# Expert weights in transfers of 2 MiB with four rows per partition, and gate and up products that take every fourth column

## The chip, the core and the metric

The kernel runs on one core of a Trainium2 chip. The metric is the time of one execution on the device in microseconds; three runs are taken and their median is given. One further execution was taken with the hardware profiler, and the rows below come from it.

## The reference

The model is two blocks on a sequence of 256 tokens of width 1024, all in f32. The first is two layers (a short convolution and a block attention, each followed by an attention to a memory of 256 rows and a gated feed-forward of width 2816). The second is one layer whose gates and shifts come from a modulation vector, with a gated delta rule branch and a latent attention branch side by side, and then a mixture of experts in which each expert chooses its tokens. The change touches only this last part and what prepares its gain and bias:

```python
def expert_choice_ffn(h, w_router, w_gate, w_up, w_down):
    bsz, s, d = h.shape
    cap = CAPACITY_FACTOR * s // N_EXPERTS          # 32 tokens for each of 16 experts
    aff = jax.nn.softmax((h @ w_router).astype(jnp.float32), axis=-1)
    gate, idx = lax.top_k(aff.transpose(0, 2, 1), cap)
    idx_flat = idx.reshape(bsz, N_EXPERTS * cap)
    xe = jnp.take_along_axis(h, idx_flat[..., None], axis=1).reshape(bsz, N_EXPERTS, cap, d)
    hid = jax.nn.silu(jnp.einsum('becd,edf->becf', xe, w_gate)) * jnp.einsum('becd,edf->becf', xe, w_up)
    ye = jnp.einsum('becf,efd->becd', hid, w_down) * gate[..., None].astype(h.dtype)
    out = jnp.zeros_like(h).at[jnp.arange(bsz)[:, None], idx_flat].add(ye.reshape(bsz, N_EXPERTS * cap, d))
    return out
```

Each of w_gate, w_up and w_down has 16 matrices of 1024 x 1024 f32, 4 MiB each: 192 MiB in all. The h that goes in is the normalised row times a gain (1 + sc2) g_ffn and plus a bias sh2, which come from the modulation.

## The kernel before, in words

Every engine has its own list of operations, written out by hand in program order, and semaphores between the lists. The dense layers stream their weights through a ring of four places: SP loads 1 MiB, ScalarE and VectorE split it into two parts (lines 243 and 250), TensorE multiplies (lines 424 to 426 and 440 to 442).

The expert weights take another way. They are cut into 192 chunks of 1 MiB: chunk j of a matrix is its rows 256j to 256j+255, two consecutive rows (8 KiB) per partition. `order()` gives the sequence: the four gate chunks and the four up chunks of an expert, then the four down chunks of the expert before it. There are 22 places of 8 KiB per partition (`wexp`), scattered over SBUF where earlier buffers come free; chunk n goes to place n mod 22. `load_expert` (line 2498) issues one chunk on SP's queue. The first 22 wait for the earlier owners of their places: three in `early_experts`, four beside the chunks of w_out (`next_experts`), the rest in `sp_experts`. From chunk 22 on SP waits until TensorE has used the chunk that lies in the place (`e_used`, raised once per chunk).

`expert_chunk` (line 2718) multiplies a chunk. The 32 chosen tokens of the expert are the stationary operand, 32 columns wide, and the weights are the moving one; the 1024 output columns are cut into four groups of 256, each of which goes to its own 32 columns of the array and its own 32 partitions of PSUM, so that four products run side by side. An f32 product leaves two records in the trace, so a chunk (two rows k, four groups c) leaves 16. The group c is the 256 consecutive columns from 256c on:

```python
dst[32 * c:32 * c + 32, :], lhs(2 * j + kk), wexp[n_ % NSLOT][:, kk, c * W4:(c + 1) * W4]
```

Which rows of a matrix lie in which partition sets what goes with them. Since partition p holds rows 2p and 2p+1 of a chunk, the gathered input (line 2735, products of the split rows with the 0/1 selection) takes every second column of each 256, and so do the turned hidden rows (line 2809), the gain and the bias (`xgain`, `xbias`, made in `modulation_rows`, lines 1228 to 1247, and from `vpair`, lines 927 to 934).

The order of the work around it: SP's queue holds the loads in the order of the chunks; TensorE's list first has the products with w_out, the router, filler products that nobody reads (`unread`, line 2565), then 16 gathers for two halves of the experts. The first four gate chunks stand between gathers (`first_gate`), the rest behind them (`pe_experts`). For each expert it then goes: gate and up; down of the expert before; turning the hidden rows. In the last two experts fillers stand behind each chunk. After the last down product the last output product (line 2827) and the final norm follow (`finish`).

Of the kernel before, what the change touches and what calls it, by code (L numbers as in the profile page):

```python
# [87 lines left out]
def build(nc, A, out):  # L88
# [423 lines left out]
    vpair = place("vpair", [12, 256], F32, offset=F0 + 34368)  # L512
# [19 lines left out]
    def load_vectors(e):  # L532
        for n_, k_ in VROWS[1:]:
            src = A[n_]
            flat = src.rearrange(" ".join("abc"[:len(src.shape)]) + " -> (" + " ".join("abc"[:len(src.shape)]) + ")")
            e.dma_start(vrow[vat[n_]:vat[n_] + k_, 0, :], flat.rearrange("(k p) -> k p", p=P)).then_inc(misc, 16)
        w5 = A["conv_w_2"][0].rearrange("w (k p) -> (w k) p", p=P)
        e.dma_start(vrow[0:CONV2 * 24, 1, :], w5).then_inc(misc, 16)
        e.dma_start(vrow[0:48, 2, :], A["b_mod_2"].rearrange("a (k p) -> (a k) p", p=P)).then_inc(misc, 16)
        for j, v_ in enumerate((A["b_mod_2"][:, 3 * D:4 * D], A["b_mod_2"][:, 4 * D:5 * D], A["g_ffn_2"])):  # L540
            e.dma_start(vpair[4 * j:4 * j + 4, :], v_.rearrange("a (c n) -> (a c) n", c=4)).then_inc(misc, 16)
# [390 lines left out]
    by_pair = V0[:, 296:320].rearrange("p (h j c) -> p j c h", h=2, j=3)  # L932
    for j, dst in enumerate((bpair[:, 0:8], bpair[:, 8:16], xgain)):
        dve.do(lambda e, j=j, dst=dst: e.tensor_copy(dst.rearrange("p (c h) -> p c h", h=2), by_pair[:, j, :, :]))
# [291 lines left out]
    def modulation_rows(prepared):  # L1226
# [16 lines left out]
        pv = X[0][:, 2 * P:4 * P].rearrange("p (h c v) -> p v c h", h=2, c=4)  # L1243
        ch2 = lambda v_: v_.rearrange("p (c h) -> p c h", h=2)
# [1213 lines left out]
    for c in range(1, 4):  # L2458
# [9 lines left out]
        for _ in half:  # L2468
# [6 lines left out]
    NSLOT = 22  # L2475
    first = st.n + 4
    ring_at = [sbuf_at[f"{n_}{(first + i) % RING}"] for i in range(RING) for n_ in ("w_raw", "w_hi")]
    wexp = [place(f"w_exp{i}", [P, 2, D], F32, offset=at)
            for i, at in enumerate((F0 + 24576, F0 + 32768, A0 + 16384, A0 + 24576, A0 + 32768, S0, S0 + 24576,
                                    S0 + 8192, S0 + 16384, A0, A0 + 8192, *ring_at, A0 + 40960, XN, sbuf_at["x"]))]  # L2480
    e_in = [nc.alloc_semaphore(f"expert_in{s_}") for s_ in range(NSLOT)]

# [13 lines left out]
    def load_expert(e, n_):  # L2496
        name, x_, j = list(order())[n_]
        e.dma_start(wexp[n_ % NSLOT][:, :, :],
                    A[name][0][x_][256 * j:256 * j + 256, :].rearrange("(p k) n -> p k n", k=2)).then_inc(e_in[n_ % NSLOT], 16)
# [211 lines left out]

    def expert_chunk(e, name, x_, j, dst, lhs):

        n_ = chunk_at[name, x_, j]
        e.wait_ge(e_in[n_ % NSLOT], 16 * (n_ // NSLOT + 1))
# [33 lines left out]
    NCH = 12 * E  # L2749
# [4 lines left out]
    def sp_experts(e):  # L2754
        for n_ in range(7, NCH):
            if n_ == 7:
                e.wait_ge(*t_merged)
            elif 11 <= n_ < 19:
                e.wait_ge(S["chunk_used"], RING + first - 4 + (n_ - 11) // 2 + 1)
            elif n_ == 19:  # L2760
                e.wait_ge(*t_x1)
            elif n_ == 20:
                e.wait_ge(*t_rows[1])
            elif n_ == 21:
                e.wait_ge(*t_held)
                e.wait_ge(*x_read[1])
            elif n_ >= NSLOT:
                e.wait_ge(e_used, n_ - NSLOT + 1)
            load_expert(e, n_)
    sp.raw(sp_experts)  # L2770

    def pe_experts(e):
# [11 lines left out]
        def down(x_):  # L2784
# [9 lines left out]
            for j in range(4):  # L2794
                expert_chunk(e, "w_down_2", x_, j, into[:, 0:W4], lambda k: hT[x_ % 2][:, k % 2, (k // 2) * C:(k // 2 + 1) * C])
# [5 lines left out]
        def turn_hidden(x_):  # L2801
# [6 lines left out]
            for c in range(2):  # L2808
                ins = e.transpose(XT[:, c * P:(c + 1) * P], hx[x_ % 2][:, :].rearrange("p (q h) -> p h q", h=2)[:, c, :], ident[:, :])
# [146 lines left out]
```

## Time and profile before

| what | value |
|---|---|
| three runs | 1763.61, 1770.14, 1771.63 us (median 1770.14) |
| profiled execution | 1778.02 us |
| its span, first to last instruction | 1776.3 us |
| mean granted TensorE clock | 0.937 |
| TensorE busy | 1583.8 us (89%) |
| DMA traffic over the span | 417 MB, 235 GB/s |
| loads of expert weights | 192 of 1 MiB, 26.6 to 27.0 us from issue to landing (median) |

The span is cut into 40 slices in the page, so a slice is 44.4 us. The busy share of an engine is an average over stages with different limits; the stage of the expert weights fills the last 12 slices.

### The profile page before, as it was taken

How to read it: one execution, taken by the hardware profiler on the slowest of the kernel's cores; microseconds unless marked ns; L12 is line 12 of the kernel's file. 1: busy time of each engine (PE TensorE's matmuls, PEld its weight loads, DVE VectorE, ACT ScalarE, POOL GpSimd, SP SyncE). 2: the span in 40 equal slices, each digit the busy share in tenths (PEclk: the TensorE clock that was granted, in tenths of full speed). 3: DMA queues.
4: the chain of work that ended last, by engine and by line, in shares of the span. 5: the costliest groups of instructions: out<-in, count | busy, mean ns of one | idle time of the engine just before them, and what ended most of it. 6: DMA issues, size and time to landing. Idle time of an engine off the chain costs nothing.

```text
span 1776.3 us, 35258 instructions
## 1 busy us (share of the span) xinstructions
PE 1583.8 (89%) x14826; PEld 1317.4 (74%) x14826; DVE 865.3 (49%) x1248; ACT 661.2 (37%) x884; POOL 143.3 (8%) x188
## 2 busy tenths in 40 slices
PE   8999999999999999999989799899999666666677
PEld 8999899988989989988888689789885222222223
DVE  5765466645655556564667589866651000000001
ACT  5445354435444435543545644534442000000001
POOL 5700000000000000000105001121110000000000
PEclk9999999999999999999999999999999776777779
DMA  7765556775735666655544144102699999999997
GB/s 247 252 200 186 183 155 189 218 255 165 262 120 178 231 186 200 182 175 174 148 123 149 58 143 143 50 27 73 239 412 403 421 421 421 420 421 421 420 421 304
DMA packets 254141, 417.17 MB, mean 235 GB/s; under 512 B 15102, under 2 KB 215345, under 8 KB 229425
## 3 DMA queue, kind: packets, MB, share of 16 engines
q1 hardware_dynamic: 253825, 414.59, 65.4%
q8 instruction: 109, 1.79, 0.4%
q10 hardware_dynamic: 176, 0.53, 0.1%
q14 instruction: 31, 0.25, 0.0%
HBM read 414.04 MB, written 1.05 MB: 234 GB/s over the span
## 4 chain that ended last, share of the span: by engine, by line
issue 47%; PE 41%; DVE 5%; POOL 4%; ACT 3%; DMA 0%; DVEq 0%; POOLq 0%; ACTq 0%; SPq 0%
PE bank L424 4%; PE bank L425 4%; PE bank L426 4%; PE bank L440 2%; PE bank L442 2%; PE bank L441 2%; PE bank L1878 2%; DVE cy L1427 1%; PE bank L1079 1%; PE bank L1078 1%; PE bank L1077 1%; PE bank L759 1%; PE bank L452 1%; POOL ang L908 1%; POOL ang L909 1%
## 5 line engine op out<-in xcount | busy, mean ns | idle before, releaser
L250 DVE TENSOR_TENSOR w_lo<-w_raw,w_hi 128x2048 fp32r<-128x2048 f32 (+2 forms) x178 | 400.8, 2254 | 252.7 <-ACT w_hi L243 252.6
L243 ACT ACTIVATE w_hi<-w_raw 128x2048 fp32r<-128x2048 f32 (+2 forms) x178 | 334.0, 1880 | 155.6 <-DMA w_raw<-in_ffn_w_down_dram 57.7
L424 PE MATMUL bank<-h_hi,w_hi 128*128 128x256 f32 x1168 | 328.0, 281 | 5.1 <-DVE h_lo L637 3.8
L425 PE MATMUL bank<-h_lo,w_hi 128*128 128x256 f32 x1168 | 327.2, 280 | 0.0
L426 PE MATMUL bank<-h_hi,w_lo 128*128 128x256 f32 x1168 | 327.2, 280 | 0.0
L2718 PE MATMUL bank<-w_exp,xeT 128*32 128x256 f32 x2048 | 170.9, 473 | 79.9 <-DMA w_exp<-in_w_up_dram 51.3
L424 PEld LDWEIGHTS bank<-h_hi,w_hi 128*128 128x128 f32 x1168 | 222.8, 191 | 6.2 <-issue 6.1
L426 PEld LDWEIGHTS bank<-h_hi,w_lo 128*128 128x128 f32 x1168 | 219.6, 188 | 0.0
L425 PEld LDWEIGHTS bank<-h_lo,w_hi 128*128 128x128 f32 x1168 | 219.4, 188 | 0.0
L2718 PEld LDWEIGHTS bank<-w_exp,xeT 128*32 128x32 f32 x2048 | 65.7, 128 | 177.6 <-DMA w_exp<-in_w_up_dram 84.3
L2718 PE MATMUL bank<-w_exp,hT 128*32 128x256 f32 x1024 | 93.9, 504 | 47.6 <-DMA w_exp<-in_w_down_dram 47.6
L2885 DVE TENSOR_TENSOR hx<-sg,bank 128x256 f32<-128x256 f32 x16 | 6.7, 421 | 255.2 <-ACT sg L2857 255.2
L2718 PEld LDWEIGHTS bank<-w_exp,hT 128*32 128x32 f32 x1024 | 34.5, 134 | 104.4 <-DMA w_exp<-in_w_down_dram 62.0
L440 PE MATMUL bank<-w_hi,a_hi 128*128 128x256 f32 x384 | 107.9, 281 | 1.1 <-issue 1.1
L442 PE MATMUL bank<-w_hi,a_lo 128*128 128x256 f32 x384 | 107.2, 279 | 0.0
L441 PE MATMUL bank<-w_lo,a_hi 128*128 128x256 f32 x384 | 107.2, 279 | 0.0
L2857 ACT ACTIVATE sg<-bank 128x256 f32<-128x256 f32 x16 | 6.1, 383 | 256.8 <-PE bank L2718 256.8
L2893 DVE TENSOR_TENSOR ye<-bank,gt 32x256 f32<-32x256 f32 x64 | 26.9, 420 | 135.3 <-PE bank L2718 134.6
L440 PEld LDWEIGHTS bank<-w_hi,a_hi 128*128 128x128 f32 x384 | 72.0, 188 | 1.4 <-issue 1.3
L441 PEld LDWEIGHTS bank<-w_lo,a_hi 128*128 128x128 f32 x384 | 72.1, 188 | 0.1
L442 PEld LDWEIGHTS bank<-w_hi,a_lo 128*128 128x128 f32 x384 | 72.0, 188 | 0.0
L1079 PE MATMUL bank<-w_hi,a_lo 128*128 128x512 f32 x176 | 69.4, 394 | 0.0
(539 smaller groups left out, 3084.8 us busy)
## 6 DMA issues: line engine op xcount, KB each, us to landing
w_exp<-in_w_gate_dram SPq DMA_DIRECT2D x64, 1024.0 KB, 26.6
w_exp<-in_w_up_dram SPq DMA_DIRECT2D x64, 1024.0 KB, 26.6
w_exp<-in_w_down_dram SPq DMA_DIRECT2D x64, 1024.0 KB, 27.0
w_raw<-in_ffn_w_gu_dram SPq DMA_DIRECT2D x88, 512.0 KB, 5.0
w_raw<-in_w_in_dram SPq DMA_DIRECT2D x54, 512.0 KB, 4.8
w_mod<-in_w_mod_dram SPq DMA_DIRECT2D x24, 1024.0 KB, 7.1
w_raw<-in_ffn_w_down_dram SPq DMA_DIRECT2D x44, 512.0 KB, 4.2
w_raw<-in_mem_w_kv_dram SPq DMA_DIRECT2D x32, 512.0 KB, 4.6
```

Source lines behind the costliest of these rows:

```text
L243: e.activation(whi[slot][:, 0:w], raw[slot][:, 0:w], ACT.Copy).then_inc(S["hi_ready"], 1)
L250: e.tensor_tensor(wlo[slot][:, 0:w], raw[slot][:, 0:w], whi[slot][:, 0:w].bitcast(F32), ALU.subtract).then_inc(S["lo_ready"], 1)
L424: e.matmul(dst, whi[slot][:, lo:hi_], bh[:, k, :], start=begin, stop=False)
L425: e.matmul(dst, whi[slot][:, lo:hi_], bl[:, k, :], start=False, stop=False)
L426: ins = e.matmul(dst, wlo[slot][:, lo:hi_], bh[:, k, :], start=False, stop=end)
L440: e.matmul(dst, bh[:, k, xs], w0, start=(k == 0), stop=False)
L441: e.matmul(dst, bh[:, k, xs], w1, start=False, stop=False)
L442: ins = e.matmul(dst, bl[:, k, xs], w0, start=False, stop=(k == kts - 1))
L1079: ins = e.matmul(dst, xl, w0, start=False, stop=(k == 2 * n - 1))
L1878: tok = pe.do(lambda e, cs=cs, s_=s_: e.matmul(out_bank[cs, s_ * 64:s_ * 64 + 64], lhs[cs, s_, :], rhs[cs, s_, :], start=True, stop=True), *w)
L2718: ins = e.matmul(dst[32 * c:32 * c + 32, :], lhs(2 * j + kk), wexp[n_ % NSLOT][:, kk, c * W4:(c + 1) * W4], start=(j == 0 and kk == 0), st ...
L2893: ins = e.tensor_tensor(ye[32 * (x_ % 4):32 * (x_ % 4) + 32, x_ // 4 % 2, c * W4:(c + 1) * W4], from_[32 * c:32 * c + 32, 0:W4], gt[32 * c ...
```

## The change

Two neighbouring chunks of a matrix become a pair: 512 rows, of which partition p holds the four rows 4p to 4p+3, 16 KiB in a run. The 22 places are regrouped into 11 pairs (`pair_of`): ten are two places that lie side by side in SBUF, the eleventh is two places apart. A pair is one transfer of 2 MiB, except for the first 22 chunks, for pairs that go to the eleventh, split place, and for the very last pair: these are loaded as two halves of 1 MiB, each with two of a partition's four rows. The first 22 halves are issued in the order in which the places come free, as before, but the chunk that belongs to a place is now another (`chunk_of`), so they are not issued in the order of their use. SP waits for both chunks of a pair to be used before it loads the next. TensorE waits for the pair's semaphore.

With four rows to a partition, everything that goes with the rows is taken in fours: the gathered input takes every fourth column of each 512, gain and bias likewise. For the hidden rows the change does it on the other side: in gate and up products, group c is no longer 256 consecutive columns but the columns 4q + c, and the hidden rows can then be turned without a step; down products keep consecutive columns. In `modulation_rows` two transposes become eight products of 64 output partitions into another bank, and the three VectorE operations on them become six, on half the partitions each.

```diff
-    pairs = vpair[:, :].rearrange("r (p h) -> r h p", h=2)
-    for h in range(2):
-        t = pe.do(lambda e, h=h: e.transpose(V0[:, 296 + 12 * h:308 + 12 * h], pairs[:, h, :], ident[0:12, 0:12]))
+    fours = vpair[:, :].rearrange("r (p h) -> r h p", h=4)
+    for h in range(4):
+        t = pe.do(lambda e, h=h: e.transpose(V0[:, 296 + 6 * h:302 + 6 * h], fours[:, h, :], ident[0:6, 0:6]))
...
-        for h in range(2):
-            tp = pe.do(lambda e, h=h: e.transpose(X[0][:, (2 + h) * P:(3 + h) * P], mrow[:, :].rearrange("p (q h) -> p h q", h=2)[:, h, :],
-                                                  ident[:, :]))
+        for h in range(4):
+            for a_ in range(2):
+                t4 = pe.do(lambda e, h=h, a_=a_: e.matmul(X[3][64 * a_:64 * a_ + 64, h * P:(h + 1) * P],
+                                                          mrow[:, :].rearrange("p (q h) -> p h q", h=4)[:, h, :], ident[:, :],
+                                                          start=True, stop=True), xfree[3])
...
-        t = dve.do(lambda e: e.tensor_tensor(ch2(xbias), pv[:, 4, :, :], ch2(bpair[:, 8:16]), ALU.add), tp, t)
-        t = dve.do(lambda e: e.scalar_tensor_tensor(out=xgain, in0=xbias, scalar=1.0, in1=xgain, op0=ALU.add, op1=ALU.mult), t)
-        t = dve.do(lambda e: e.tensor_tensor(ch2(xbias), pv[:, 3, :, :], ch2(bpair[:, 0:8]), ALU.add), t)
+        for a_ in range(2):
+            fs = slice(64 * a_, 64 * a_ + 64)
...
+            t = dve.do(lambda e, pv=pv, ch4=ch4: e.tensor_tensor(ch4(xbias), pv[:, 4, :, :], ch4(bpair[:, 8:16]), ALU.add), t4, t)
+            t = dve.do(lambda e, fs=fs: e.scalar_tensor_tensor(out=xgain[fs, :], in0=xbias[fs, :], scalar=1.0, in1=xgain[fs, :],
+                                                               op0=ALU.add, op1=ALU.mult), t)
+            t = dve.do(lambda e, pv=pv, ch4=ch4: e.tensor_tensor(ch4(xbias), pv[:, 3, :, :], ch4(bpair[:, 0:8]), ALU.add), t)
...
+    def pair_rows(m):
+        name, x_, j = list(order())[2 * m]
+        return A[name][0][x_][256 * j:256 * j + 512, :].rearrange("(p k) n -> p k n", k=4)
+
+    def load_half(e, n_, sem):
+        e.dma_start(wexp[n_ % NSLOT][:, :, :], pair_rows(n_ // 2)[:, n_ % 2 * 2:n_ % 2 * 2 + 2, :]).then_inc(sem, 16)
+
+    def load_expert(e, i):
+        load_half(e, chunk_of[i], e_in[chunk_of[i]])
+
+    def load_pair(e, m):
+        if m == NCH // 2 - 1:
+            for hf in range(2):
+                load_half(e, 2 * m + hf, e_in[hf])
+        elif m % NP == NP - 1:
+            for hf in range(2):
+                load_half(e, 2 * m + hf, pair_in[m % NP])
+        else:
+            e.dma_start(wpair[m % NP][:, :, :], pair_rows(m)).then_inc(pair_in[m % NP], 16)
...
+    def group_of(name, row, c):
+        return row[:, c * W4:(c + 1) * W4] if name == "w_down_2" else row.rearrange("p (q c) -> p c q", c=4)[:, c, :]
...
-                               wexp[n_ % NSLOT][:, kk, c * W4:(c + 1) * W4],
+                               group_of(name, wexp[n_ % NSLOT][:, kk, :], c),
...
-                X[b][:, 0:H * C], part[:, t_, (k // 2) * 256:(k // 2 + 1) * 256].rearrange("p (q h) -> p h q", h=2)[:, k % 2, :], Sa[:, t_, cs],
+                X[b][:, 0:H * C], part[:, t_, (k // 4) * 512:(k // 4 + 1) * 512].rearrange("p (q h) -> p h q", h=4)[:, k % 4, :], Sa[:, t_, cs],
...
-            elif n_ >= NSLOT:
-                e.wait_ge(e_used, n_ - NSLOT + 1)
-            load_expert(e, n_)
+            load_expert(e, i)
+        for m in range(NP, NCH // 2):
+            e.wait_ge(e_used, 2 * (m - NP) + 2)
+            load_pair(e, m)
...
-                ins = e.transpose(XT[:, c * P:(c + 1) * P], hx[x_ % 2][:, :].rearrange("p (q h) -> p h q", h=2)[:, c, :], ident[:, :])
+                ins = e.transpose(XT[:, c * P:(c + 1) * P], hx[x_ % 2][:, c * P:(c + 1) * P], ident[:, :])
```

## Rows read from the trace of the kernel before

**Rows 1.** The page, the span in 40 equal slices.

```profile
PE   8999999999999999999989799899999666666677
PEclk9999999999999999999999999999999776777779
DMA  7765556775735666655544144102699999999997
```

**Rows 2.** The chain that ended last: start us, us, what.

```profile
1326.05 444.46 issue
```

**Rows 3.** Windows by stage.

```profile
core 0: us, PE busy (x) PEld busy (x) DVE busy (x) ACT busy (x) POOL busy (x), PEclk, DMA share, GB/s
1265.00:1340.00 75.00, 70.72 (x579) 63.72 (x578) 39.55 (x70) 31.98 (x49) 6.24 (x5) 1.00 1.03 402
...
1400.00:1440.00 40.00, 24.96 (x262) 8.80 (x264) 2.11 (x5) 0.77 (x2) 0.00 (x0) 0.74 1.01 421
1440.00:1750.00 310.00, 211.00 (x2066) 80.28 (x2067) 21.44 (x51) 8.05 (x21) 0.00 (x0) 0.75 1.01 421
```

**Rows 4.** Waits of SP, 1200 to 1777: us in total, times, longest us.

```profile
SPq L2498 <- PE bank L2718: 203.3, 153, 4.5
```

**Rows 5.** The page: packets; queue 1 (packets, MB, share of 16 engines); one row of issues.

```profile
DMA packets 254141, 417.17 MB, mean 235 GB/s; under 512 B 15102, under 2 KB 215345, under 8 KB 229425
...
q1 hardware_dynamic: 253825, 414.59, 65.4%
...
w_exp<-in_w_gate_dram SPq DMA_DIRECT2D x64, 1024.0 KB, 26.6
```

**Rows 6.** Timeline of TensorE in the tail: start us, us.

```profile
1752.31 1.07 PE L2718 MATMUL bank<-w_exp,hT 128*32 128x256 f32 x16 [1.80 <-DMA w_exp<-in_w_down_dram]
...
1754.80 1.94 PE L2718 MATMUL bank<-w_exp,hT 128*32 128x256 f32 x16 [0.22 <-DMA w_exp<-in_w_down_dram]
...
1758.73 1.07 PE L2718 MATMUL bank<-w_exp,hT 128*32 128x256 f32 x16
...
1764.67 1.07 PE L2718 MATMUL bank<-w_exp,hT 128*32 128x256 f32 x16 [0.85 <-DMA w_exp<-in_w_down_dram]
...
1766.82 3.60 PE L2827 MATMUL bank<-ye,GT 128*128 128x512 f32 x8
```

**Rows 7.** Timeline of TensorE behind the gathers: chunks 4 to 7.

```profile
1342.06 3.66 PE L2718 MATMUL bank<-w_exp,xeT 128*32 128x256 f32 x64
```

**Rows 8.** Timeline of SP's issues there, and times to landing from 1320 to 1345.

```profile
1326.08 0.81 SPq L2498 DMA_DIRECT2D w_exp<-in_w_gate_dram  x2
...
1331.13 2.74 SPq L2498 DMA_DIRECT2D w_exp<-in_w_gate_dram  x2
...
1343.19 1.94 SPq L2498 DMA_DIRECT2D w_exp<-in_w_up_dram  x2
...
DMA to landing us min/median/max: 5.3/7.6/9.6
```

**Rows 9.** A window of one microsecond, columns as in rows 3.

```profile
1344.00:1345.00 1.00, 1.00 (x24) 0.63 (x20) 0.00 (x0) 0.24 (x2) 0.00 (x0) 1.00 0.89 205
```

**Rows 10.** Single lines: weight loads in sequence and with a step, ns min/median/max.

```profile
L1230 PEld LDWEIGHTS bank<-ident,mrow x2: 137/138/138, 790.6 to 790.7; 128*128 128x128 f32 x2
...
L1232 PEld LDWEIGHTS bank<-ident,mrow x2: 195/201/207, 790.8 to 790.9; 128*128 128x128 f32 x2
...
L2735 PEld LDWEIGHTS bank<-Sa,h_hi x32: 193/195/198, 1328.0 to 1341.6; 128*128 128x128 f32 x32
```

**Rows 11.** The page, groups: busy us, mean ns of one, idle before.

```profile
L424 PEld LDWEIGHTS bank<-h_hi,w_hi 128*128 128x128 f32 x1168 | 222.8, 191 | 6.2 <-issue 6.1
```

**Rows 12.** Timeline of all engines at the modulation: start us, us.

```profile
793.73 0.17 DVE L1245 TENSOR_TENSOR small<-bank,bpair 128x8 f32<-128x8 f32 x1
793.93 0.17 DVE L1246 SCALAR_TENSOR_TENSOR small<-small 128x8 f32<-128x8 f32 x1
...
795.05 1.95 PE L1254 MATMUL bank<-mexp,sel 128*128 128x512 f32 x4 [2.04 <-DVE gt L1256]
```

More of the change, by code:

```diff
@@ L511, in build @@
     vrow = place("vrow", [P, 3, P], F32, offset=F0 + 32832)
-    vpair = place("vpair", [12, 256], F32, offset=F0 + 34368)
+    vpair = place("vpair", [6, 512], F32, offset=F0 + 34368)
     def col(name, k=0):
@@ L540, in load_vectors @@
         for j, v_ in enumerate((A["b_mod_2"][:, 3 * D:4 * D], A["b_mod_2"][:, 4 * D:5 * D], A["g_ffn_2"])):
[L541 removed]
+            e.dma_start(vpair[2 * j:2 * j + 2, :], v_.rearrange("a (c n) -> (a c) n", c=2)).then_inc(misc, 16)
         e.dma_start(invf[:, :], A["inv_freq"]).then_inc(pos_in, 16)
@@ L2474, in build @@
     E, C = N_EXP, CAP
-    NSLOT = 22
+    NSLOT, NCH = 22, 12 * E
     first = st.n + 4
     ring_at = [sbuf_at[f"{n_}{(first + i) % RING}"] for i in range(RING) for n_ in ("w_raw", "w_hi")]
-    wexp = [place(f"w_exp{i}", [P, 2, D], F32, offset=at)
-            for i, at in enumerate((F0 + 24576, F0 + 32768, A0 + 16384, A0 + 24576, A0 + 32768, S0, S0 + 24576,
-                                    S0 + 8192, S0 + 16384, A0, A0 + 8192, *ring_at, A0 + 40960, XN, sbuf_at["x"]))]
+    NP = NSLOT // 2
+    free_in_order = (F0 + 24576, F0 + 32768, A0 + 16384, A0 + 24576, A0 + 32768, S0, S0 + 24576,
+                     S0 + 8192, S0 + 16384, A0, A0 + 8192, *ring_at, A0 + 40960, XN, sbuf_at["x"])
+    pair_of = [next((i, j) for i in range(NSLOT) for j in range(NSLOT)
+                    if free_in_order[i] == a_ and free_in_order[j] == a_ + 8192)
+               for a_ in (F0 + 24576, A0 + 16384, S0, S0 + 16384, A0, *(min(free_in_order[i], free_in_order[i + 2]) for i in (11, 12, 15, 16)), A0 + 32768)] + [(20, 21)]
+    chunk_of = {i: 2 * m + hf for m, two in enumerate(pair_of) for hf, i in enumerate(two)}
+    wpair = [place(f"w_exp_pair{m}", [P, 4, D], F32, offset=free_in_order[two[0]]) for m, two in enumerate(pair_of[:-1])]
+    wexp = [wpair[m][:, 2 * hf:2 * hf + 2, :] for m in range(NP - 1) for hf in range(2)]
+    wexp += [place(f"w_exp{i}", [P, 2, D], F32, offset=free_in_order[i]) for i in pair_of[-1]]
     e_in = [nc.alloc_semaphore(f"expert_in{s_}") for s_ in range(NSLOT)]
+    pair_in = [nc.alloc_semaphore(f"expert_pair_in{m}") for m in range(NP)]
     def order():
@@ L2494, in order, with landed @@
             yield "w_down_2", E - 1, j
[L2496 to L2499, printed above, removed]
+    def pair_rows(m):
[14 more added lines that the diff above has]
+            e.dma_start(wpair[m % NP][:, :, :], pair_rows(m)).then_inc(pair_in[m % NP], 16)
+    def landed(n_):
+        m = n_ // 2
+        if n_ < NSLOT:
+            return e_in[n_], 16
+        if m == NCH // 2 - 1:
+            return e_in[n_ % 2], 32
+        return pair_in[m % NP], (32 if m % NP == NP - 1 else 16) * (m // NP)
     def early_experts(e):
@@ L2754, in sp_experts @@
     def sp_experts(e):
-        for n_ in range(7, NCH):
-            if n_ == 7:
+        for i in range(7, NSLOT):
+            if i == 7:
                 e.wait_ge(*t_merged)
-            elif 11 <= n_ < 19:
-                e.wait_ge(S["chunk_used"], RING + first - 4 + (n_ - 11) // 2 + 1)
-            elif n_ == 19:
+            elif 11 <= i < 19:
+                e.wait_ge(S["chunk_used"], RING + first - 4 + (i - 11) // 2 + 1)
+            elif i == 19:
                 e.wait_ge(*t_x1)
-            elif n_ == 20:
+            elif i == 20:
                 e.wait_ge(*t_rows[1])
-            elif n_ == 21:
+            elif i == 21:
                 e.wait_ge(*t_held)
                 e.wait_ge(*x_read[1])
-            elif n_ >= NSLOT:
-                e.wait_ge(e_used, n_ - NSLOT + 1)
-            load_expert(e, n_)
+            load_expert(e, i)
+        for m in range(NP, NCH // 2):
+            e.wait_ge(e_used, 2 * (m - NP) + 2)
+            load_pair(e, m)
     sp.raw(sp_experts)
@@ L2794, in down @@
             for j in range(4):
-                expert_chunk(e, "w_down_2", x_, j, into[:, 0:W4], lambda k: hT[x_ % 2][:, k % 2, (k // 2) * C:(k // 2 + 1) * C])
+                expert_chunk(e, "w_down_2", x_, j, into[:, 0:W4], lambda k: hT[x_ % 2][:, k // 4, (k % 4) * C:(k % 4 + 1) * C])
                 if x_ == E - 2:
```

12 lines of the change are left out of this document (6 added, 6 removed).

## The prediction

> **What bounds the kernel now.** I read the slices of the page first. For the first 28 of the 40 slices TensorE is busy nine tenths and the DMA engines anything from nothing to nine tenths; from slice 29 on, the stage of the expert weights, the picture turns over: the DMA engines stand at nine tenths and TensorE falls to six or seven [rows 1]. The chain that ended last is of no use in this stage: it has one step of 444.46 us called "issue" from 1326.05 to the tail [rows 2], because it does not follow the transfer queue. So the windows by stage decide: from 1400 to 1750 us all 16 DMA engines are busy (share 1.01) and move 421 GB/s, in both windows alike, while TensorE works 25 of 40 us at three quarters of its clock [rows 3]. The queue is never short of a place either: SP waits 203 us there for TensorE to hand places back [rows 4], and a load lands 26.6 us after its issue, ten loads deep [rows 5]. A load of 1.0486 MB at 421 GB/s takes 2.49 us, and 2.49 us is also the distance at which TensorE's waits for the last loads end (1752.31, 1754.80) [rows 6]. The end of the kernel is therefore: the moment at which the DMA engines begin to run full (about 1265), plus the bytes over the rate, plus every hole in the DMA traffic, plus what TensorE does after the last load (from 1764.67). The change has to be priced in these four places, and in TensorE's path before 1265.
>
> **The rate: 77 loads of 2 MiB.** Of 192 chunks the first 22 still come singly, as do the two chunks of the split place in each round (7 pairs) and the last pair. 96 - 11 - 7 - 1 = 77 pairs become one transfer. The transfers before have 8 KiB per packet: 24,716 packets (254,141 less 229,425) are of 8 KB or more, and 192 loads times 128 partitions are 24,576 [rows 5]. What one packet costs comes from two sums. Queue 1 was busy 65.4% of 16 x 1776.3 us = 18,587 us. The expert loads have 201.3 MB of it, at 421 GB/s and share 1.01: 7,728 us in 24,576 packets. The rest is 213.3 MB and 10,859 us in 229,249 packets. Solving for a price per MB and one per packet gives 36.8 us per MB (16 engines: 435 GB/s) and 13.1 ns per packet. Some 3 ns of that overlap the next packet, since the share reads 1.01 and not 1.00 of 314 ns, so 10 ns count in time. A full pair has 8 packets of 16 KiB per engine instead of 16 of 8 KiB: 8 x 10 = 80 ns saved, times 77 = **-6.2 us**. Bounds: 0 (if a long row is cut again into pieces of 8 KiB, nothing is saved), and -12.4 us (if 154 MiB ran at the full 435 GB/s: 154 x (2.491 - 2.410)). The 402 GB/s of 1265 to 1340, where rows of 1 KiB for w_out are mixed in [rows 3], say that packets do cost something, so I take the middle one. The Trainium skill (DMA: Bandwidth & Descriptors, Why small descriptors are slow) has about 3 cycles a packet and 32 bytes of descriptor, which at its fabric clock is some 4.7 ns; by that the gain would be only about 2.9 us.
>
> **The hole around 1344.** This is where the release in pairs is felt. Chunks 20 and 21 are issued by 1326.5, chunk 22 at 1331.13 when chunk 0 is used, 23 at 1333.5, and so on, and 26 only at 1343.19, since the first gate chunks lie between the gathers and chunk 4 comes behind them at 1342.06 [rows 7, 8]. Loads in this stretch land 5.3 us after issue at least, so a load begins some 1.6 us after its issue when nothing stands ahead, and there the traffic falls to 205 GB/s for a microsecond [rows 8, 9]. Before, chunk 25 is through at about 1344.2. Going back four loads at 402 GB/s, chunk 21 is through at about 1333.8. After, chunks 22 and 23 wait for chunk 1 (1333.5) and start at 1335.1: through at 1340.1; 24 and 25 wait for chunk 3 (1338.35), through at 1345; 26 and 27 wait for chunk 5, 1344.06 instead of 1343.19, and start at 1345.7 instead of 1344.8. **+0.9 us**, and whatever delays chunk 5 on TensorE adds to it one for one. After that pairs are released every 1.7 us against 4.9 us of transfer, and nothing is lost.
>
> **Columns with a step of four.** The moving operand of gate and up is now read at a step of 16 bytes. No matmul before reads a moving operand with a step; the nearest rows are weight loads: the same 128x128 of f32 takes 138 ns in sequence and 201 ns with a step of 8 bytes, 1.4 to 1.5 times, while the gather's split weights with a step of two take 195 ns [rows 10], against 191 ns for split weights in sequence [rows 11]. A chunk is 16 matmul records in 0.9 us at full clock (64 in 3.66) [rows 7]. I take 1.4 times, +0.36 us a chunk, since these are unsplit f32 as in the first pair of rows; the bounds are no cost and, if the four column groups had to read one after the other, 4 times. In the steady stage this is covered: (2 x 1.3 + 0.9) / 3 is 1.2 us a chunk against 2.49, and even at the low clock (1.94 us a chunk at 1754.80 [rows 6]) it is 2.5, with the clock free to rise. Up to chunk 5 it is not: six chunks, 6 x 0.36 = **+2.2 us**. The gather's 64 weight loads go from a step of two to four: between 0 and 64 x 57 ns = 3.6 us; the split weights show 4 ns for step two, so **+0.3 us**. The Trainium skill (SBUF — State Buffer, the door of the DMA port swizzle, its note on cachelines of 16 bytes) wants at least two hits per line for full speed, which this read of f32 no longer has; that speaks against the change, and its consequence is the first rival.
>
> **The tail.** Chunk 186 landed for 1752.31, 187 for 1754.80; now both land with 187. TensorE then has, in a row: 186 (1.9, the low clock) and four filler products (1.2), 187 (1.1) and four (0.9), turning the hidden rows until 188 can start (1.2), 188 to 190 with fillers (1.6, 1.9, 1.5): 11.3 us, read from the starts of the chunks [rows 6] and of the fillers between them. The last half lands 9.9 us after that pair. **+1.3 us**; bounds 0 and, if the clock stays at 1.2 GHz there and in the 3.60 us of the output product, +8.
>
> **Modulation, near 791 us.** Two transposes go, eight f32 products of 128 columns come (16 records at some 60 to 110 ns, 1 to 1.8 us). The engine behind them waits 2.04 us for VectorE anyway [rows 12], which covers them; without that cover they would cost up to 1.8. VectorE's chain gets three more operations of 0.17 us with 0.03 between them, ahead of the gt products on which that wait rests [rows 12]: **+0.6 us**. The vector transposes early on (four for two, of six rows) are under 0.2 us. The step in the transposes of hidden rows goes away: 2 x 0.06 us, off the path. SP issues fewer transfers; it waits anyway. The new order of the first 22 loads puts chunk 18 at the fifth place and brings chunks 4 to 7 later, but all of them stand ahead of the issue at 1326.08 [rows 8], and chunk 4 is first used at 1342.06 [rows 7].
>
> **Sum.** -6.2 + 0.9 + 2.2 + 0.3 + 1.3 + 0.6 = -0.9 us. The profiled execution took 1778.0 us around a span of 1776.3, so it would be 1777.1; the median of the three runs is 1770.1, and it would be **1769.2**. About 0.5% (8.9 us) is what a measurement of this kernel can tell from no change, so this is "within".
>
> **Rivals.** (1) *The strided read becomes slow enough to show*, the other side. With d us more per gate or up chunk, the start costs 6d. Near the end each of expert 15's eight gate and up chunks carries 1.0 us of fillers too, so 0.9 + 1.0 + d exceeds 2.49 from d = 0.5 to 0.6 on, and eight of them pile up 8(d - 0.5), of which the four down chunks win back 1.9. At d = 1.8 (3 times) that is 10.8 + 8.5 against the 2.2 in the sum: +17, **1786**. Slower by 0.5% from about d = 1.3, 2.4 times. For it: sequence against step in the weight loads, and four column groups reading at once. Against: the split weights hardly mind. Chance 0.20. (2) *The strided read is free*: -3.1 us, **1767**. 0.20. (3) *Long rows save nothing*, the change not doing what it says: +5.3, **1775**. 0.12. (4) *Long rows run at 435 GB/s and the read is free*: -12.4 + 0.9 + 0.3 + 1.3 + 0.6 = -9.3, **1761**, just faster. For it only the round figure that the solution gave. 0.10. (5) *The clock falls in the tail* because TensorE now idles once per pair for longer: +7 to +8, **1777**, at times over the line. 0.06. The forecast keeps 0.32.
>
> Faster: (4), and a little of (2) = 0.13. Slower: (1) and some of (3) and (5) = 0.23. Within: 0.64. The range takes in (4) and (1) up to three times: 1759 to 1786; the forecast's own is 1764 to 1775.
>
> **What would show it.** The steady windows: 427 to 428 GB/s if a packet costs 10 ns, 421 if nothing is saved. The number of packets: 9,856 fewer. Sixteen matmuls of a gate chunk at full clock: 1.3 us against 0.9. The traffic between 1333 and 1346: two holes of about a microsecond. The start of the last chunk, against the last landing: over a microsecond late. The prediction falls if rates in the steady windows go down (16 KiB rows in step across partitions), or if a gate chunk takes over 2.2 us.

## The result, and the profile after

The changed kernel took 1785.7 us (median of nine runs) against 1770.2 us for the kernel before (nine runs): a ratio of **1.0081 [1.0065, 1.0097]**, 14.3 us slower. The prediction was 1769.2 us and no change to be told. The ratios here and below rest on undisturbed executions alone; two of the twelve of e12 took 2991.6 and 3770.7 us, for a reason that no trace shows, and stand outside its ratio.

The two profiled executions lie only 3.5 us apart in their spans (1779.8 against 1776.3), because that of before was a late one: at the modulation, near 790 us, it stood 5.8 us behind the other, and there the two kernels have run the same work but for two tiny transposes more in the changed kernel. So I compare stretches that begin at a common mark. The mark for the stage of the experts is the first start of the operation that writes xn behind the last residual (line 2649 before, line 2686 after). This is the view of that line in the changed kernel:

```profile
core 0 of [0], span 1779.8 us
...
L2686 ACT ACTIVATE xn<-x,small x2: 1132/1132/1133, 1314.9 to 1317.0; 128x1024 f32<-128x1024 f32 x2
```

From 1314.9 to the end of the span are 464.9 us. Before they were 456.2 us (1320.1 to 1776.3): **+8.7 us** in this stage.

The page of the changed kernel, slices, packets and queue 1, answering to [rows 1] and [rows 5]:

```profile
PE   9999999999999999999989799899999977686778
PEclk9999999999999999999999999999999999998999
DMA  7755657765736557645453244002898999999996
...
DMA packets 243040, 417.15 MB, mean 234 GB/s; under 512 B 13864, under 2 KB 214095, under 8 KB 228181
...
q1 hardware_dynamic: 242725, 414.59, 64.8%
```

Three windows of the changed kernel (columns as in [rows 3]): two of the places where traffic all but stops, and the steady stage. Behind them the same steady window of the kernel before:

```profile
1330.00:1332.00 2.00, 2.00 (x17) 0.60 (x10) 0.00 (x0) 0.44 (x1) 0.00 (x0) 1.00 0.10 41
1348.00:1350.00 2.00, 2.00 (x21) 0.60 (x16) 0.00 (x0) 0.64 (x2) 0.00 (x0) 1.00 0.00 0
...
1450.00:1700.00 250.00, 178.19 (x1659) 62.38 (x1652) 18.01 (x43) 6.69 (x18) 0.00 (x0) 0.93 1.01 427
```

```profile
1450.00:1700.00 250.00, 167.63 (x1608) 60.62 (x1605) 18.50 (x44) 6.52 (x17) 0.00 (x0) 0.72 1.01 421
```

The reader sees three things. The packets are fewer by 11,101: 9,856 because 16 KiB now go in one packet instead of two, and the rest are small ones that the 77 transfers fewer no longer need. The steady rate is 427 GB/s for 421, as forecast. But between 1328 and 1352 the traffic falls away three times, near 1331, 1340 and 1349, while TensorE is busy without a break in the windows shown; the middle time it does not stop (33 GB/s in its lowest microsecond). And in the steady stage TensorE works longer for the same products: 178 of 250 us at a granted clock of 0.93, against 168 us at 0.72.

TensorE's timeline of the changed kernel at the first gate chunks, answering to [rows 7], and SP's issues there, answering to [rows 8]:

```profile
1325.77 2.00 PE L2758 MATMUL bank<-w_exp_pair,xeT 128*32 128x256 f32 x16
1327.69 0.51 PE L2775 MATMUL bank<-Sa,h_hi 128*128 128x256 f32 x1
1328.04 0.39 PE L2775 MATMUL bank<-Sa,h_lo 128*128 128x256 f32 x1
1328.27 0.40 PE L2775 MATMUL bank<-Sa,h_hi 128*128 128x256 f32 x1
...
1346.46 7.45 PE L2758 MATMUL bank<-w_exp_pair,xeT 128*32 128x256 f32 x64
```

And the first gate chunk of the kernel before, with the gather's products behind it:

```profile
1330.00 1.07 PE L2718 MATMUL bank<-w_exp,xeT 128*32 128x256 f32 x16 [0.15 <-ACT xeT L2738]
1331.00 0.39 PE L2735 MATMUL bank<-Sa,h_hi 128*128 128x256 f32 x1
1331.23 0.28 PE L2735 MATMUL bank<-Sa,h_lo 128*128 128x256 f32 x1
1331.35 0.28 PE L2735 MATMUL bank<-Sa,h_hi 128*128 128x256 f32 x1
```

SP's issues in the changed kernel:

```profile
1331.82 0.33 SPq L2528 DMA_DIRECT2D w_exp_pair<-in_w_gate_dram  x1
...
1339.85 0.33 SPq L2528 DMA_DIRECT2D w_exp_pair<-in_w_up_dram  x1
...
1350.36 0.33 SPq L2528 DMA_DIRECT2D w_exp_pair<-in_w_up_dram  x1
```

Sixteen products of a gate chunk take 1.92 us from the first to the next operation (1325.77 to 1327.69), and 1.00 us before (1330.00 to 1331.00); 64 of them take 7.45 us for 3.66. The gather's products follow each other at 0.23 us, and before at 0.12. All of this lies ahead of chunk 5, whose use releases the third pair: it is issued 35.5 us after the mark (1350.36), and chunk 26 before was issued 23.1 us after it. The transfer queue has run dry by then. I call *missing traffic* the sum of (1 less GB/s over the steady rate) over the windows of one microsecond that lie below the steady rate in the first 60 us behind the mark: **14.6 us** after, 2.6 us before.

### The profile page after: what moved, and what is told of

Its sections match the earlier page's. It is cut to its first block, busy times and chain, and to the rows that moved or that the text cites. A ratio compares the mean times of both kernels' runs of the same rounds, so it can differ in the third digit from the quotient of the medians.

```text
span 1779.8 us, 35217 instructions
## 1 busy us (share of the span) xinstructions
PE 1628.3 (91%) x14842; PEld 1323.0 (74%) x14842; DVE 865.6 (49%) x1251; ACT 662.7 (37%) x884; POOL 149.5 (8%) x188
## 4 chain that ended last, share of the span: by engine, by line
issue 47%; PE 40%; DVE 5%; POOL 4%; ACT 3%; DMA 1%; DVEq 0%; POOLq 0%; SPq 0%; ACTq 0%
PE bank L424 4%; PE bank L425 4%; PE bank L426 4%; PE bank L440 2%; PE bank L442 2%; PE bank L441 2%; PE bank L1884 2%; PE bank L1077 1%; PE bank L1079 1%; PE bank L1078 1%; PE bank L759 1%; DVE cy L1433 1%; POOL ang L908 1%; PE bank L452 1%; POOL ang L909 1%
## 5 line engine op out<-in xcount | busy, mean ns | idle before, releaser
L2758 PE MATMUL bank<-w_exp_pair,xeT 128*32 128x256 f32 x1888 | 223.3, 631 | 40.4 <-DMA w_exp_pair<-in_w_gate_dram 22.5
L2758 PEld LDWEIGHTS bank<-w_exp_pair,xeT 128*32 128x32 f32 x1888 | 65.7, 126 | 181.1 <-issue 134.1
L2758 PE MATMUL bank<-w_exp_pair,hT 128*32 128x256 f32 x928 | 64.9, 425 | 37.6 <-DMA w_exp_pair<-in_w_down_dram 37.6
L2758 PEld LDWEIGHTS bank<-w_exp_pair,hT 128*32 128x32 f32 x928 | 32.1, 120 | 72.1 <-DMA w_exp_pair<-in_w_down_dram 31.9
L1077 PE MATMUL bank<-w_hi,a_hi 128*128 128x512 f32 x176 | 69.7, 396 | 0.0
```

Source lines behind the costliest of these rows:

```text
L1077: e.matmul(dst, xh, w0, start=(k == 0), stop=False)
```

## The experiments

Each of e1 to e12 was timed against the kernel before on the same chip, with twelve executions of its own (e11 with six); e13 and e14 were only profiled. The kernels e1 to e6, e10 and e14 leave out the reordering that one side of a product would need, so they do the same amount of work but do not compute the reference. The table has the ratio with its interval; the stage of the experts from the mark to the end in the profiled execution; the missing traffic; the steady rate; and the idle time marked issue in front of TensorE's first product of line 465.

| run | ratio | stage, us | missing, us | GB/s | line 465, us |
|---|---|---|---|---|---|
| before | 1 | 456.2 | 2.6 | 421 | 1.3 |
| the change | 1.0081 [1.0065, 1.0097] | 464.9 | 14.6 | 427 | 2.5 |
| e1_flat_groups | 1.0029 [1.0009, 1.0049] | 456.9 | 8.6 | 427 | 2.4 |
| e2_flat_gather | 1.0037 [1.0018, 1.0056] | 460.1 | 9.1 | 427 | 2.6 |
| e3_flat_both | 1.0001 [0.9983, 1.0020] | 454.0 | 5.2 | 427 | 2.3 |
| e4_before_step | 1.0030 [1.0010, 1.0049] | 462.1 | 7.0 | 421 | 1.3 |
| e5_flat_halves | 1.0031 [1.0016, 1.0046] | 461.3 | 3.9 | 421 | 2.7 |
| e6_before_modulation | 1.0030 [1.0011, 1.0050] | 456.7 | 1.5 | 421 | 2.9 |
| e7_no_steps | 1.0019 [1.0003, 1.0036] | 456.9 | 6.2 | 427 | 2.7 |
| e8_no_steps_ends | 1.0006 [0.9990, 1.0022] | 454.1 | 5.0 | 426 | 2.7 |
| e9_more_records | 1.0016 [1.0001, 1.0032] | 456.8 | 1.4 | 421 | 1.5 |
| e10_fewer_records | 1.0011 [0.9989, 1.0033] | 457.4 | 2.4 | 421 | 1.2 |
| e11_after_no_fillers | 1.0061 [1.0039, 1.0082] | 465.6 | 15.0 | 427 | 2.9 |
| e12_best | 0.9993 [0.9972, 1.0014] | 453.8 | 3.9 | 427 | 1.4 |
| e13_seam48 | not timed | 456.3 | 1.3 | 421 | 2.6 |
| e14_seam24 | not timed | 457.1 | 1.3 | 421 | 1.6 |

The row of a stage is one profiled execution. How far such a number scatters can be read from six kernels whose work in this stage is the same (before, e6, e9, e10, e13, e14): 456.2 to 457.4 us, and 1.3 to 2.6 us of missing traffic.

**e1, e2, e3: reads in order, one at a time and both.** On the changed kernel:

```diff
-        return row[:, c * W4:(c + 1) * W4] if name == "w_down_2" else row.rearrange("p (q c) -> p c q", c=4)[:, c, :]
+        return row[:, c * W4:(c + 1) * W4]
```

```diff
-                X[b][:, 0:H * C], part[:, t_, (k // 4) * 512:(k // 4 + 1) * 512].rearrange("p (q h) -> p h q", h=4)[:, k % 4, :], Sa[:, t_, cs],
+                X[b][:, 0:H * C], part[:, t_, k * P:(k + 1) * P], Sa[:, t_, cs],
```

> This is the changed kernel with one part taken back: gate and up products read consecutive columns again (so the hidden columns come out in another order than the down products want; the amount of work is the same). Theory 1, that reads with a step of 16 bytes on TensorE cost the time: a gate chunk takes 1.0 us instead of 1.9, which takes 6 us out of the hole in the DMA traffic before 1352 and the backlog of about 4 us out of the tail, so about 10 us less than the changed kernel, 1.003 of the kernel before. Theory 2, that the hand-over in pairs costs the time: no more than 1 us less, still 1.008.

> The changed kernel with the gather alone reading consecutive columns of the rows (so the gathered input has its columns in another order; the amount of work is the same). Theory 1: 64 products at 0.12 us instead of 0.23, 7 us less in the hole, 1.004 to 1.005 of the kernel before, with the gate chunks still at 1.9 us and the tail still late. Theory 2: still 1.008.

> The changed kernel with consecutive reads both in the gate and up products and in the gather (order of columns as in the two runs before, the same amount of work); transfers, places and hand-over are those of the change. Theory 1: all of the loss goes and the gain of the rate of 6 us stays, less about 3 us for holes, tail and modulation: 0.998 of the kernel before, 427 GB/s in the steady windows. Theory 2: still 1.005 or more.

Each alone takes somewhat over half of the loss away, both together all of it. The 0.998 expected for both was a little too low: the measured interval begins at 0.9983. The columns in order (e1) save 8.0 us of the stage, 6.0 of them in missing traffic; the gather in order (e2) saves 4.8, 5.5 in missing traffic. Expected were 10 and 7 us. The weight loads of the gather, single line, with the step of four (e1) and in order (e2), ns min/median/max:

```profile
L2775 PEld LDWEIGHTS bank<-Sa,h_hi x32: 307/329/332, 1328.9 to 1348.2; 128*128 128x128 f32 x32
```

```profile
L2775 PEld LDWEIGHTS bank<-Sa,h_hi x32: 186/187/192, 1322.7 to 1340.0; 128*128 128x128 f32 x32
```

With a step of two they took 195 ns [rows 10]: for these split weights a step of 8 bytes is next to free (195 ns for 187), and one of 16 bytes costs three quarters more (329 ns).

**e4: the step alone, on the kernel before.** One line of `expert_chunk` of the kernel before:

```diff
-                               wexp[n_ % NSLOT][:, kk, c * W4:(c + 1) * W4],
+                               (wexp[n_ % NSLOT][:, kk, c * W4:(c + 1) * W4] if name == "w_down_2" else wexp[n_ % NSLOT][:, kk, :].rearrange("p (q c) -> p c q", c=4)[:, c, :]),
```

> The kernel before with one part of the change alone: gate and up products read every fourth column (the hidden columns come out in another order than the down products want; the same amount of work). Loads of 1 MiB and single hand-over stay. Theory 1: a gate chunk takes 1.9 us, +6 us in the hole, and +1 to 2 us in the tail since eight chunks of 2.83 us with fillers stand against 2.49: 1.004 to 1.005 of the kernel before. Theory 2: 1.000.

1.0030 [1.0010, 1.0049], near what the theory of the slow reads had (1.004 to 1.005), and against the theory of the hand-over in pairs, since this kernel has no pairs. The stage is 5.9 us longer. The 1 to 2 us expected in the tail did not come: here the last chunk starts 0.7 us behind the last traffic, as before. Its timeline of TensorE at the first gate chunks:

```profile
1325.18 2.00 PE L2718 MATMUL bank<-w_exp,xeT 128*32 128x256 f32 x16
1328.52 2.00 PE L2718 MATMUL bank<-w_exp,xeT 128*32 128x256 f32 x16 [0.18 <-ACT xeT L2738]
```

**e5: the rate.** On e3, each full pair is loaded as two halves on the pair's semaphore:

```diff
-            e.dma_start(wpair[m % NP][:, :, :], pair_rows(m)).then_inc(pair_in[m % NP], 16)
+            for hf in range(2):
+                load_half(e, 2 * m + hf, pair_in[m % NP])
```

> As the run with both reads consecutive (same order of columns as there), but each full pair is loaded in two transfers of 1 MiB with 8 KiB per partition, handed over together as before. Theory, that the gain comes from fewer and longer packets (10 ns each): the steady windows fall from 427 back to 421 GB/s and the stage of the experts gets 6.2 us longer, 1.0035 of the kernel before. Rival, that the rate rose because SP hands out places in pairs or issues less often: 427 GB/s stays, 1.000.

The steady window of e3 and that of e5:

```profile
1450.00:1700.00 250.00, 151.00 (x1666) 68.81 (x1670) 18.49 (x44) 6.51 (x17) 0.00 (x0) 0.79 1.01 427
```

```profile
1450.00:1700.00 250.00, 149.59 (x1628) 67.47 (x1632) 16.83 (x40) 6.13 (x16) 0.00 (x0) 0.77 1.01 421
```

The rate goes back to 421 and the stage is 7.3 us longer. So the gain is real and it comes with the longer packets (and the fewer small ones), not with the way in which places are handed out. Of the 7.3 us, 6.0 are a later end of the traffic (447.5 for 441.5 us behind the mark, in windows of 0.1 us). The other 1.3 us lie in the tail, where e5 shows what the prediction had described: chunk 186 waits for the landing of its pair, TensorE then takes 1.93 us over it for the 1.07 of the others (granted clock 0.51 in those 1.9 us), and the last chunk starts 11.3 us later, 2.2 us behind the last traffic (0.9 in e3):

```profile
1759.41 1.93 PE L2759 MATMUL bank<-w_exp_pair,hT 128*32 128x256 f32 x16 [2.28 <-DMA w_exp_pair<-in_w_down_dram]
...
1770.67 1.07 PE L2759 MATMUL bank<-w_exp_pair,hT 128*32 128x256 f32 x16
```

**e6, e9, e10, e13, e14: the modulation.** In e1, e2 and e3 the timed ratios lie 2 to 4 us above what the profiled stages say. e6 is the kernel before with the change in `modulation_rows`, `vpair` and what reads it, and nothing else:

> The kernel before with only the part of the change in the modulation and its vectors (eight products and six VectorE operations for two transposes and three; gain and bias then come out in an order that the old gather does not want; the same amount of work). If this part costs what its rows say, +0.8 us, 1.0005 of the kernel before. If the 2 to 4 us by which the timed ratios of the three runs on the changed kernel lie above their profiled stages of the experts come from here, 1.002.

It was 1.0030, 5.3 us, though the stretch from the modulation to the seam is 67.4 us long for 66.6: the 0.8 us of its rows. The next thing that stands out is a wait of TensorE that the profile marks issue, that is, one for which it names nobody. Timeline of e6:

```profile
935.42 0.36 PE L465 MATMUL bank<-w_hi,h_hi 128*128 128x256 f32 x1 [2.87 <-issue]
```

It is 2.3 to 2.9 us in every kernel with the modulation part and with 32 fillers at the seam, and 1.3 before and in e4. The runs that follow vary how many TensorE products stand ahead of it, counted in records of the trace (an f32 product of the modulation leaves two, a transpose or a filler one). e9 repeats two transposes of the kernel before, 14 more products:

```diff
-        for h in range(2):
+        for h in 8 * (0, 1):
             tp = pe.do(lambda e, h=h: e.transpose(X[0][:, (2 + h) * P:(3 + h) * P], mrow[:, :].rearrange("p (q h) -> p h q", h=2)[:, h, :],
```

e10 is e6 with fewer fillers at the seam, e14 is e6 with `unread_at_seam(24)`, and e13 is the kernel before with `unread_at_seam(48)`:

```diff
-    unread_at_seam(32)
+    unread_at_seam(16)
```

> The kernel before with the two transposes of the modulation at line 1232 repeated eight times, 14 more TensorE instructions of the same kind and nothing else. Every profile of a kernel with the modulation part of the change has a stall of 2.3 to 2.9 us in front of the first product of line 465 near 935 us, which the profile calls issue, and neither profile without that part has it. Theory, that the stall comes and goes with the number of TensorE instructions ahead of it: it appears here, and the time is +0.8 and +2.6 us, 1.002. Rival, that it belongs to the modulation's operations themselves: no stall, 1.0005.

> The kernel before with the modulation part of the change, and 16 instead of 32 filler products at the seam behind it, so that as many TensorE products stand ahead of line 465 as before the change (columns in the wrong order for the old gather, as before). Theory of the count: the stall at line 465 is gone, and the ratio falls from 1.003 to 1.0005 or 1.001. Rival: it stays, 1.003. The fillers lie in a wait, so fewer of them save nothing by themselves.

> The kernel before with 48 instead of 32 filler products at the seam, nothing else: 16 TensorE products more ahead of line 465, as many as the modulation part of the change adds. Theory, that the stall marked issue in front of line 465 depends on the number of TensorE instructions ahead of it: it is 2.3 to 2.9 us long here instead of 1.3. Rival, that it depends on the modulation's own operations: 1.3.

> The kernel before with the modulation part of the change and 24 filler products at the seam: 8 products more ahead of line 465 than before. Theory of the count: 1.3 to 1.5 us, as with 0 and with 14 more. Rival: 2.3 to 2.9.

The waits of TensorE in this stretch, from the profiles of e6, e9, e10, e13 and e14:

```profile
PE bank L465 <- issue: 2.9, 1, 2.9
```

```profile
PE bank L465 <- issue: 1.5, 1, 1.5
```

```profile
PE bank L465 <- issue: 1.2, 1, 1.2
```

```profile
PE bank L465 <- issue: 2.6, 1, 2.6
```

```profile
PE bank L465 <- issue: 1.6, 1, 1.6
```

By the number of TensorE products ahead of this line beyond those of before: 0 gives 1.3 (before, e4), 1.2 (e10) and 1.4 (e12), 8 gives 1.6, 14 gives 1.5, 16 gives 2.6 (e13), 2.9 (e6) and 2.3 to 2.9 in the others. My expectation for e9 missed by two products. But e13, which has nothing of the modulation and only fillers more, has the long wait, and e10, which has all of the modulation, has not: the wait goes with the count of the products ahead, not with what they are. What happens at the count is not shown; the profile only says that TensorE waited for nothing that it records.

Nor is it shown that this wait costs the kernel its length. From the modulation (line 1230) to the mark, the kernels with the short wait took 528.5 to 530.6 us and those with the long one 529.5 to 534.1, so the two groups overlap; e6 took the most (534.1 for 529.4 before), and the changed kernel 530.0. The intervals of e6 and of e10, which has the short wait (1.0011 [0.9989, 1.0033]), overlap too. Counting 0.8 us for the rows, 1.6 for the wait and 0.5 in the stage makes 2.9 us for e6, which is inside its interval (1.9 to 8.9 us); the rest of its 5.3 us is open.

**e11: the fillers of the last expert.** On the changed kernel, in `gate_up`:

```diff
-                    if x_ == E - 1:
-                        unread(e, XG[E % 2], 4, Sa[:, 0, 0:384])
```

> The changed kernel without the four filler products behind each gate and up chunk of the last expert (work that nobody reads). Theory, that the tail is late because 1.92 us of product and 0.9 us of fillers are more than the 2.45 us in which a chunk lands: the backlog is gone, TensorE waits for the last loads again, and the last chunk starts 4 us sooner against the start of the stage: 1.006 of the kernel before. Rival, that the backlog comes from the hand-over in pairs, or that the clock falls without the fillers: nothing won, 1.008.

The changed kernel's tail, timeline of TensorE, answering to [rows 6]:

```profile
1743.34 2.00 PE L2758 MATMUL bank<-w_exp_pair,xeT 128*32 128x256 f32 x16
1745.26 0.98 PE L2602 MATMUL bank<-Sa 128*128 128x384 f32 x4
1746.17 2.00 PE L2758 MATMUL bank<-w_exp_pair,xeT 128*32 128x256 f32 x16
...
1754.64 1.07 PE L2758 MATMUL bank<-w_exp_pair,hT 128*32 128x256 f32 x16
...
1768.15 1.07 PE L2758 MATMUL bank<-w_exp_pair,hT 128*32 128x256 f32 x16
```

Chunks with fillers are 2.83 us apart, with no wait for a load from 1734.85 to the end. And that of e11:

```profile
1767.99 1.07 PE L2758 MATMUL bank<-w_exp_pair,hT 128*32 128x256 f32 x16 [0.83 <-DMA w_exp_pair<-in_w_down_dram]
...
1772.99 1.07 PE L2758 MATMUL bank<-w_exp_pair,hT 128*32 128x256 f32 x16
```

TensorE waits for loads again, so the backlog is gone; but the last chunk starts 454.0 us behind the mark and not sooner than in the changed kernel (453.3), because here the last loads themselves came later (traffic ends 453.1 us behind the mark for 451.2; the gather began 0.9 us later, for one). The expected 4 us did not come. Timed, it is 1.0061, below the changed kernel's 1.0081, with intervals that overlap. What the backlog is worth is read from how long after the last traffic the last chunk starts: 2.1 us in the changed kernel, 0.9 in e11 and 0.7 before, so 1.2 to 1.4 us.

**e7, e8, e12: the idea without slow reads on TensorE.** These compute the reference in full. On the changed kernel the normalised rows are laid down in fours by ScalarE, so the gather reads in order; gate and up read in order; and the hidden rows are turned by products that pick every fourth column in the stationary operand:

```diff
+            for k in range(4):
+                for a_ in range(2):
+                    ins = e.matmul(XT[64 * a_:64 * a_ + 64, k * 64:(k + 1) * 64],
+                                   hx[x_ % 2][:, :].rearrange("p (q k) -> p k q", k=4)[:, k, :],
+                                   ident[:, :].rearrange("p (j a s) -> p a j s", j=2, a=2)[:, a_, :, :], start=True, stop=True)
...
-        act.do(lambda e: e.activation(x_hi[:, t_, :], x[:, t_, :], ACT.Copy, scale=rs[:, t_:t_ + 1]), t_rs, all_used())
+        act.do(lambda e: e.activation(in_fours(x_hi[:, t_, :]), by_fours(x[:, t_, :]), ACT.Copy, scale=rs[:, t_:t_ + 1]), t_rs, all_used())
```

e8 also loads and hands over the first and the last three pairs behind the early ones chunk by chunk. e12 is e8 with ScalarE reading in order and writing with the step, and with `unread_at_seam(16)`.

> A full version of the idea without slow reads: pairs and 2 MiB as in the change; ScalarE writes the normalised rows already in fours, so the gather reads consecutive columns; gate and up read consecutive columns; the hidden rows are turned by eight small products with a step in the stationary operand, some 1 us per expert. Theory 1: as with both reads consecutive, the stage of the experts about 454 us, plus 0 to 2 us if ScalarE reads with a step of 16 bytes more slowly, plus 0.7 us for the last turning: 1.000 of the kernel before.

> The same, but the first three pairs that follow the 22 early chunks and the last three pairs are loaded as single chunks of 1 MiB and handed over singly. If the hand-over in pairs costs the rest of the hole near the first gate chunks (5.2 us of holes in the run with both reads consecutive against 2.6 before), the holes fall by about 2 us: 0.999 of the kernel before; if not, the same as without this.

> The full version with no steps in the reads of TensorE and single chunks at both ends, with two changes: ScalarE reads the rows in order and writes them in fours (before: it read with a step of 16 bytes, 2.12 us for 1.13), and 16 fillers fewer at the seam to keep the count of TensorE instructions. If ScalarE only minds the step on the side it reads, the gather starts 1 to 2.7 us sooner; with no stall at line 465 another 2.6 us: 0.998 to 0.999 of the kernel before. If writing with a step costs the same, 0.999 to 1.000.

The step has moved to ScalarE, and there it costs too, on whichever side it is. Timelines of ScalarE, e8 (step in the read) and e12 (step in the write), for an operation that took 1.13 us:

```profile
1316.98 2.11 ACT L2688 ACTIVATE xn<-x,small 128x1024 f32<-128x1024 f32 x1
```

```profile
1314.07 2.06 ACT L2688 ACTIVATE xn<-x,small 128x1024 f32<-128x1024 f32 x1
```

The gather begins 9.0 to 10.6 us behind the mark instead of 7.9. Not all of that is ScalarE's: in e2, e3, e5, e10 and e11, where ScalarE has no step, it begins 8.7 to 9.1 us behind it. In e8, with 10.6, an operation of VectorE that took 0.57 us before took 2.47, beside a subtraction of GpSimd that began with it; that the one held up the other was not tested:

```profile
1323.25 2.34 POOL L2690 TENSOR_TENSOR h_lo<-xn,h_hi 128x1024 fp32r<-128x1024 f32 x1 [1.69 <-ACT xn L2688]
1323.26 2.47 DVE L2721 TENSOR_SCALAR mk__199<-cur 16x256 f32<-16x256 f32 x1
```

The first operation with the new step also lies ahead of the mark, so the table flatters these three by some 0.5 to 0.7 us. e7 was expected at 1.000 and came at 1.0019 [1.0003, 1.0036]; e8, expected at 0.999, at 1.0006 [0.9990, 1.0022], with 1.2 us less of missing traffic than e7 for the 2 expected. e12 is the best of them: 0.9993 [0.9972, 1.0014], 2.4 us less than before in the stage (1.9 if the stage is begun one operation earlier), but not to be told from the kernel before in time.

## Why the prediction was wrong

By its own steps:

- **The rate, -6.2 us: right.** 427 GB/s was forecast and read; e5, which gives it back, ends its traffic 6.0 us later than e3. The price of 10 ns a packet, worked out from the two sums, held. The estimate of 4.7 ns worked out from the Trainium skill (DMA: Bandwidth & Descriptors, Why small descriptors are slow) would have been too little.
- **The hole, +0.9 us for the hand-over in pairs: too small, its cause not settled.** e3 has 5.2 us of missing traffic for 2.6 before, and for 1.3 to 2.4 in the other kernels with single hand-over and reads in order. Some of that is the gather's later start in that execution (8.8 for 7.9 us behind the mark), and e8, which hands the first three pairs over singly, still has 5.0.
- **Columns with a step of four, +2.2 us: here the prediction failed.** It priced the read of the moving operand at 1.4 times, from weight loads with a step of two. It is 1.92 times (1.92 us for 1.00), so the six chunks cost 5.5 us; e1 shows 6.0 in missing traffic. The mechanism, that it counts up to chunk 5 one for one and is hidden after, was right.
- **The gather, +0.3 us: the other half of the failure.** I had bounded it at 3.6 us and taken the low end, since split weights with a step of two cost 4 ns. But the change takes a step of two to one of four, and the products went from 0.12 to 0.23 us each: 5.5 us of missing traffic in e2. The bound itself was too low: its 57 ns are 195 less 138, a step of two again. The step of four costs 329 ns for 187. The line-of-16-bytes rule that I had cited, the Trainium skill's SBUF — State Buffer (Door 1: The DMA port swizzle, its note on cachelines), applied to both reads: the trace agrees with its two hits per line, at 8 bytes 195 ns and at 16 bytes 329 ns, and I set it aside for the gather. The same note has a stride of 4 fp32 as free, and there the trace differs: this is the step that cost 329 ns for 187.
- **The tail, +1.3 us: the size right, by another cause, and that is luck.** The last chunk of the changed kernel starts 2.1 us behind the last traffic for 0.7 before, 1.4 us more. But it is the backlog of the last expert, which stood in the first rival: TensorE waits for no load from 1734.85 on. The mechanism of the forecast, the landing in pairs, did not show in e3, where with reads in order the last chunk starts 0.9 us behind the last traffic; it showed in e5, with the 11.3 us that the prediction had reckoned and 2.2 us.
- **Modulation, +0.6 us: right for its rows (0.8).** 16 more products lengthen a wait at line 465 from 1.3 to 2.5 us, and the prediction had no term for that. Whether it costs time is not shown: from the seam to the mark the changed kernel took 462.6 us and the kernel before 462.8.

In the sum the hole, the columns and the gather are 12.0 us of missing traffic instead of 3.4, the rate pays 6.2 back, and the tail adds 1.4: 7.2 of the 8.7 us in the stage. With the 0.8 and, if it counts, the 1.2 ahead of the stage it is 10.7 us. The timed 14.3 us (11.5 to 17.2 by the interval) leaves 3.6 us that no row accounts for. The same sum gives, for e1 to e6, 2.6, 6.0, -0.4, 5.9, 7.3 and 2.9 us against 5.1, 6.6, 0.2, 5.3, 5.5 and 5.3 timed, so it is good to 2.5 us for one profiled execution each; the 3.6 us are more than that and stay open.

The first rival, slow enough reads, came true in kind, and at a smaller ratio than the 2.4 times that it asked for, since it kept the gather at 0.3 us. With the measured 0.92 us more a chunk its own formula gives 1774 us; the gather's 5.5 us bring it to 1779. That was a fault of the ledger: one property of the reads had been priced in two terms by two different rows, and only one of the two was varied in the rival. The outer range, 1759 to 1786, does reach the measured 1785.7, but its upper end stood for reads three times as slow and a gather at next to nothing. That it reaches so far is luck.

## What to carry to other kernels

Before rows in a partition are regrouped to lengthen transfers, list every operand that inherits the new step, on every engine, and price each by a row with that very step; here a step of 8 bytes (195 ns for 187) said nothing of one of 16 (329 ns). A queue that is full for 400 us can still run dry in the 30 us in which its first places come free. There everything that TensorE does ahead of the first releases counted nearly one for one (5.9 us of e4's stage for six chunks of 0.92 us more), though in the steady stage the same reads were hidden behind the loads. And where two kernels differ by less than a percent, compare profiled stretches from a common mark, since executions drift by several microseconds before it.

## What the runs showed of the hardware

- A step of 16 bytes in f32 costs: as moving operand of four column groups side by side 1.92 us for 1.00 a chunk of 16 records (e4 against before); as stationary split weights 329 ns for 187 (e1, e2), and 195 at 8 bytes (before); on ScalarE 2.1 us for 1.13 for 1024 elements per partition, in the read (e8) and in the write (e12) alike.
- Packets of 16 KiB ran at 427 GB/s, packets of 8 KiB at 421, on the same places with the same hand-over (e3, e5).
- TensorE has a wait near 935 us for nothing recorded, 1.2 to 1.6 us long with 0 to 14 products more ahead of it than in the kernel before (six kernels), and 2.3 to 2.9 us with 16 more (ten kernels), fillers (e13) and products of the modulation (e6) alike.
